# A pad of 16 or 24 floats ahead of the working buffers of a one-core transformer kernel

## The reference

```
# first block, two layers
x = x + short_conv_mixer(rmsnorm(x), ...)          # "conv"
x = x + swiglu(rmsnorm(x), gate, up, down)         # "ffn1", width 2816
x = x + mla_mixer(rmsnorm(x), cos, sin, ...)       # "mla", 8 heads, latent attention with rope
x = x + moe_swiglu(rmsnorm(x), router, ...)        # "moe", 8 experts, top 2, width 2048
# second block, one layer
h = h + concat(forgetting_attention, multiscale_pool) @ w_out   # "fox", 8 heads of 64
h = h + memory_attention(rmsnorm(h), rmsnorm(mem)) @ w_mem_out  # "mem", 4 heads of 128
h = h + swiglu(rmsnorm(h), gate_up, down)                       # "ffn2", width 2816
```

## Time and profile before

| | us |
|---|---|
| three runs | 1307.53, 1304.44, 1307.34 |
| median | 1307.34 |
| the profiled execution's own time | 1307.53 |
| its span in the trace | 1305.4 |

### The profile page before, as it was taken

How to read it: one execution, slowest core, us unless ns; L and a number is a source line. 1 busy time by engine, 2 the same in 40 slices (tenths; PEclk the granted TensorE clock), 3 DMA queues, 4 the chain that set the end, 5 groups by cost and what they waited for, 6 DMA issues and landing times.

```text
span 1305.4 us, 15842 instructions
## 1 busy us (share of the span) xinstructions
PE 1259.5 (96%) x6057; PEld 1035.4 (79%) x6057; DVE 927.7 (71%) x926; ACT 821.9 (63%) x905; POOL 41.8 (3%) x52
## 2 busy tenths in 40 slices
PE   7999999999999899999999999999999998999998
PEld 6887888888887788877887787768678886788887
DVE  4685555446768978898989989898777573645542
ACT  5646344337867767798788878877577665544431
POOL 4001000000000200000000000002010000000000
PEclk9999999999999999999999999999999999999999
DMA  9648655553327899999999999999683241555540
GB/s 324 231 137 279 210 186 193 163 165 124 106 105 296 346 422 396 396 392 422 394 418 399 422 400 405 407 360 392 231 290 129 98 161 65 195 192 193 164 159 33
DMA packets 89855, 339.45 MB, mean 260 GB/s; under 512 B 6267, under 2 KB 14160, under 8 KB 66128
## 3 DMA queue, kind: packets, MB, share of 16 engines
q1 hardware_dynamic: 86816, 328.64, 67.2%
q0 software_dynamic: 2816, 9.89, 2.2%
q10 hardware_dynamic: 160, 0.07, 0.0%
HBM read 332.02 MB, written 9.44 MB: 262 GB/s over the span
## 4 chain that ended last, share of the span: by engine, by line
PE 75%; DVE 12%; issue 6%; ACT 4%; DMA 3%; POOL 0%; DVEq 0%; ACTq 0%
PE bank L1905 22%; PE bank L1907 22%; PE bank L1906 22%; DVE w_lo L390 8%; PE bank L2268 1%; DMA moe_slots_in<-h,row_to 1%; ACT w_hi L385 1%; DMA raw_beside<-in_moe_w_down 1%; PE bank L2017 1%; PE bank L2277 1%; PE bank L2278 1%; PE bank L2044 1%; PE bank L2260 1%; DVE x L1197 1%; POOL moe_slots_in L610 0%
## 5 line engine op out<-in xcount | busy, mean ns | idle before, releaser
L390 DVE TENSOR_TENSOR w_lo<-raw,w_hi 128x2048 fp32r<-128x2048 f32 (+3 forms) x218 | 484.8, 2241 | 189.7 <-ACT w_hi L385 189.0
L385 ACT ACTIVATE w_hi<-raw 128x2048 fp32r<-128x2048 f32 (+3 forms) x218 | 407.6, 1878 | 205.9 <-PE bank L1907 195.9
L1905 PE MATMUL bank<-w_hi,xT_hi 128*128 128x512 f32 (+2 forms) x672 | 256.8, 382 | 4.2 <-DVE w_lo L390 2.3
L1907 PE MATMUL bank<-w_hi,xT_lo 128*128 128x512 f32 (+2 forms) x672 | 253.8, 378 | 0.0
L1906 PE MATMUL bank<-w_lo,xT_hi 128*128 128x512 f32 (+2 forms) x672 | 253.5, 377 | 0.0
L1905 PEld LDWEIGHTS bank<-w_hi,xT_hi 128*128 128x128 f32 x672 | 127.2, 189 | 28.2 <-issue 3.9
L1907 PEld LDWEIGHTS bank<-w_hi,xT_lo 128*128 128x128 f32 x672 | 126.9, 189 | 23.0
L1906 PEld LDWEIGHTS bank<-w_lo,xT_hi 128*128 128x128 f32 x672 | 127.2, 189 | 21.9
L1905 PE MATMUL bank<-w_hi,gT_hi 128*128 128x512 f32 x320 | 125.8, 393 | 2.7 <-DVE w_lo L390 2.3
L1907 PE MATMUL bank<-w_hi,gT_lo 128*128 128x512 f32 x320 | 124.7, 390 | 0.0
L1906 PE MATMUL bank<-w_lo,gT_hi 128*128 128x512 f32 x320 | 124.6, 389 | 0.0
(11 more groups left out here) (428 smaller groups left out, 1746.9 us busy)
## 6 DMA issues: line engine op xcount, KB each, us to landing
raw<-in_moe_w_gate SPq DMA_DIRECT2D x34, 1024.0 KB, 9.0
raw<-in_moe_w_up SPq DMA_DIRECT2D x34, 1024.0 KB, 7.6
raw<-in_moe_w_down SPq DMA_DIRECT2D x32, 1024.0 KB, 12.2
raw<-in_w_gate_up SPq DMA_DIRECT2D x22, 1024.0 KB, 5.2
raw_beside<-in_moe_w_down SPq DMA_DIRECT2D x18, 1024.0 KB, 12.6
raw_beside<-in_moe_w_gate SPq DMA_DIRECT2D x16, 1024.0 KB, 7.4
raw_beside<-in_moe_w_up SPq DMA_DIRECT2D x16, 1024.0 KB, 8.5
back<-in_moe_w_gate SPq DMA_DIRECT2D x14, 1024.0 KB, 7.7
```

Source lines behind the costliest of these rows:

```text
L385: nc.scalar.activation(w_hi[:, slot, :n], raw_of(i, stream, ring)[:, :n], ACT.Copy).then_inc(stream.high, 1)
L390: nc.vector.tensor_tensor(w_lo[:, slot, :n], raw_of(i, stream, ring)[:, :n], w_hi[:, slot, :n].bitcast(F32), ALU.subtract).then_inc(stream ...
L1905: mm(dst, a_hi, b_hi, start=start, stop=False)
L1907: return mm(dst, a_lo, b_hi, start=False, stop=stop)
```

## The change

The buffer that nothing uses becomes 24 floats wide and not 16, so the region begins at byte 151712 and not 151680. Every buffer behind it moves by 32 bytes: those at phase 0 go to phase 32, and the eleven named above, and the small ones beside them, go from phase 32 to phase 0. The buffers ahead of the region (`raw`, `w_hi`, `w_lo`, `x`, `raw_beside`, `xT_hi`, `xT_lo`, `junk`, `const`) stay where they are. No instruction, operand shape, wait, transfer size or place in HBM changes, and on each of the five engines the instructions stand in the same order with the same waits.

```
--- before.py
+++ after.py
@@ -36,7 +36,7 @@
 FF_GROUPS = [(i * HALF, min(HALF, FF - i * HALF)) for i in range(-(-FF // HALF))]
 CHUNK = 2048
 RING = 4
-REGION_PAD = 16
+REGION_PAD = 24
 AHEAD = 3
 FIRST_PIECES = ((0, 2), (2, 2), (4, 2), (6, 2))
 EXPERT_RING = RING + 4
```

## The result

| | before | after |
|---|---|---|
| median of the timed runs, us | 1306.34 | 1314.84 |
| lowest to highest | 1304.44 to 1307.53 | 1313.10 to 1316.45 |
| the profiled execution's own time | 1307.53 | 1318.11 |
| span of the profiled execution | 1305.4 | 1316.0 |

A fourth run of the kernel before (1305.34 us) brought its median from 1307.34 to 1306.34. The profiled execution of the kernel after is not among its four timed runs and lies 1.7 us above the highest of them.

The account below looks back on a forecast made before the run. The prediction took TensorE's matmuls to bound the kernel, with VectorE's splits setting the pace in light experts and chunk landings close behind. All terms were taken as 0, giving 1307.5 us, stated as 1307.3 against the median; range 1302.0 to 1313.5.

Parts of the forecast that it names:

- Weight loads: TensorE, 2856 matmuls with stationary operand going to phase 32: loads of 188 ns stay hidden under 227 ns, cost 0.
- the prediction's own sign: Wrong if the 127 us of an expert pair, or the matmuls' distance (0.227 us), changes by more than its third digit.
- The second: Rival: TensorE's split-type weight loads lose their cover at phase 32; at 2 ns beyond, 5.7 us, 1313.0; chance 0.03.
- The third: Faster rival: TensorE reads at one phase hinder each other, differing phases free them; 5.7 us less, 1301.6; chance 0.07.
- an address that does what no row showed: Anywhere in the kernel: a slower way that the prediction couldn't name, no size given; chance 0.04.
- The first: Rival: landing in back becomes 18% slower, light experts and scatter from h wait; 6.9 us, 1314.2; chance 0.09.
- within 0.5 of 10.8 as forecast: Light experts: the load into back that took 10.8 us was to stay within 0.5 us, a sign of no change.
- The fourth rival: Clock falls at another moment; one stretch more or less gives 1308.9 or 1305.7; counted within no change, together 0.70.
- VectorE, ScalarE and the float32 products: Splits, copies and attention's transposes and products: taken as 0, with 0 to +0.2 us for VectorE, -0.1 to +0.1 for attention.

Follow-up runs that it names:

- micro1: Rows of 60 single matmuls, network not computed, operand places, types and widths varied; split type, 512 columns: 226.7 ns at multiples of 256 bytes, 228.9 at 192, elsewhere 230 to 238.
- all32: Kernel before with a gap of 8 floats ahead of raw, so every buffer moves by 32 bytes: 1306.83 us, ratio 0.9999.
- w32: Kernel before with w_hi and w_lo alone moved by 32 bytes (stationary operands by 256): 1325.71 us, ratio 1.0146.
- moe_only: Kernel before with, of the stationary operands, only the experts' gT and eT moved, to 32 bytes from w_hi and w_lo: 1312.30 us, ratio 1.0046.
- stat_only: Kernel before, REGION_PAD still 16, gaps moving the weight products' stationary operands to phase 32: 1313.67 us, ratio 1.0055.
- rest_only: Against the kernel before: REGION_PAD 24 as in the change, gaps bringing the weight products' stationary operands back to phase 0: 1314.45 us, ratio 1.0059.
- pad80: Kernel before with REGION_PAD 80 and not 16, a distance of 256 bytes more: 1305.98 us, ratio 0.9998.

## Why the prediction was wrong

**The step that failed** is "Weight loads", with its cover of 39 ns against a difference of 1 ns, cost 0. The count was right (2856 products get a stationary operand from the region), the price was not: 6.5 ns each where TensorE sets the pace, while the load keeps its 188 ns. By the prediction's own sign it is wrong: the distance of the matmuls went from 0.227 to 0.233 us and the pair of experts from 127.3 to 129.1. Two things were wrong with the comparison.

The rows could not show it. `fqT` with `fkT`, and `qkT` with itself, are operands that stand a multiple of 256 bytes apart, both at the cheap distance, and they are float32 with at most 256 columns, for which micro1 finds no price at 32 bytes, the one distance tried. I had written down that rows existed for float32 alone, and took them because an element has the same 4 bytes. That is the point where the range should have opened.

And the question was put wrongly. I asked for the place of each buffer modulo 64, one operand at a time, and the quantity that counts is of two operands together. A load of 188 ns under a matmul of 227 looks free as a duration; it isn't shown to be free as long as no row of its type and width has another distance between its operands; the transposes of the earlier trace rows have one, and they are float32 with 128 columns. The price is read from the starts of the matmuls. That it belongs to the load and not to the matmul isn't shown.

**The rivals.** The second (weight loads lose their cover) had the right products and, at 2 ns each, 1313.0 us, but not the mechanism: nothing comes out from under the 227 ns, since the load stays at 188. The third said that it matters how the two operands stand to each other, and it had the sign reversed: the same place is the cheap one, and 32 bytes apart is dear. It held that the Trainium skill's page SBUF — State Buffer (Who interferes with whom) leaves it nothing, as TensorE's two read ports are independent there. all32, w32 and the single matmuls show a price that follows the places of the two operands, 226.7 against 233.3 ns with TensorE alone at work, which that rule of the Trainium skill doesn't cover; whether the price arises at these ports is not shown. The way it went, an address that does what no row showed, had been given 0.04. The first (landing in `back`) is refuted by the landings above and by all32, and not needed in moe_only. One load of that kind in the second light expert did take longer, 11.8 us and not within 0.5 of 10.8 as forecast, and ScalarE waited for it by 0.45 us, in after:

```profile
711.06 1.92 ACT L385 ACTIVATE w_hi<-back 128x2048 fp32r<-128x2048 f32 x1 [0.45 <-DMA back<-in_moe_w_up]
713.56 1.91 ACT L385 ACTIVATE w_hi<-raw 128x2048 fp32r<-128x2048 f32 x1 [0.57 <-DMA raw<-in_moe_w_down]
```

It is followed by a wait of 0.57 us as in the earlier trace rows, and the stretch of that pair lost only what the others did. From the second expert's down product to the last light one, ScalarE's waits for transfers come to 2.5 us after and 3.1 before.

**The fourth rival is in the numbers,** on the faster side. 2064 products (96 with `yT`, 528 with `ffn`, five times 288) by 6.5 ns are 13.4 us, and the median rose by 8.5. The profiled traces differ by 10.6, after the clock gave back 1.64 in one place. On the chip of the first runs the mean granted clock was 0.9965 for the kernel before (17 runs), 0.9983 for stat_only and 0.9978 for rest_only (6 each), so there the slower kernels lost less time to the lower level. It is no rule: w32, the slowest of all, had 0.9968 in its four runs and the kernel before 0.9967 beside it (23 runs). One run of each had a mean clock of 1.000: 1303.46 us for before, 1312.34 for stat_only and 1312.80 for rest_only, a loss of 8.9 and 9.3 us.

Where the remaining 4 us went is settled in part only. The 192 products in the first expert's gate and up should cost 1.25 us, and from the first to the last start they took 45.9 us after and 45.4 before. The last row of the experts should lose 1.9 us; it went from 87.1 us to 87.5 in moe_only, stat_only and w32, to 88.3 in rest_only and to 89.1 in after, where ScalarE waited 3.21 us for a late chunk and had waited 1.98. That row changes from trace to trace by itself: it is 86.8 us in all32 and 91.4 in pad80, whose matmuls cost the same, and 6.8 us at the lower clock account for 3.4 of these 4.6.

**Right** were VectorE, ScalarE and the float32 products (0.98 us for a head's values before in the earlier trace rows, and 0.98 after, from 1037.97 to 1038.95):

```profile
1037.97 0.59 PE L2572 MATMUL bank<-fox_tmp,z 128*128 128x256 f32 x2
...
1038.95 0.39 PE L2563 MATMUL bank<-fkT,fqT 128*128 128x128 f32 x2
```

## What to carry to other kernels

For products of the split type with 496 to 512 columns (those tried with this loss in full), let the stationary and the moving operand start a multiple of 256 bytes apart: 226.7 ns against 233.3, 2.9% of such a matmul and 0.5 to 1.5% of this kernel's time, for a pad. Measure a matmul from start to start, and before a row is used to say that an address doesn't matter, ask whether it has the same type, the same width and another distance. Any small buffer put in ahead of such an operand can spoil it, so the pad belongs where it is recomputed when the layout changes.

## What the runs showed of the hardware that was not expected

- The period is 256 bytes (512 and 1024 cost what 0 does, 264 what 8 does), and within it 192 is better than the rest (228.9 ns), while 200 and 184 are not (230.6, 232.0).
- bf16 with 512 columns costs 215.8 ns, the split type 226.7 at best and float32 858.3, the latter two with a weight load of 188 to 190 ns, bf16 with one of 98.
- A narrower stationary operand makes the matmul dearer at distance 0, not cheaper: 226.7 ns with 128 columns, 231.7 with 32.
- The mean granted clock was 0.9983 for stat_only and 0.9965 for the faster kernel before it, but 0.9968 and 0.9967 for w32 and its fellow: whether slower matmuls raise it is not shown.
